# One stage for the projections and the attention of the first block's mixer

## The reference, cut to what matters

```python
def hybrid_mixer(h, w_in, pos_ck, w_ck1, w_ck2, pos_cv, w_cv1, w_cv2, w_out, cos, sin):
    proj = h @ w_in                       # 2840 columns
    q_n, kv_n, gate_n, moba = jnp.split(proj, ...)
    ...
    o_nsa = nsa_mixer(q_n, *kv_n, gate_n, ...)     # 8 heads of 64: compressed, selected, window
    o_moba = moba_mixer(*qkv_m, cos, sin)          # 8 heads of 64
    return jnp.concatenate([o_nsa, o_moba], axis=-1) @ w_out

# nsa_mixer
    kc = gelu((blocks(k_cmp) + pos_ck) @ w_ck1) @ w_ck2    # 15 blocks of 32 tokens, hidden width 256
    vc = gelu((blocks(v_cmp) + pos_cv) @ w_cv1) @ w_cv2
    p_c = masked_softmax(q @ kc.T * scale)
    o = g0 * (p_c @ vc) + g1 * o_slc + g2 * o_win          # both others use rotated q and k
```

## Time and profile before

| | |
|---|---|
| median of 3 runs | 2489.86 us (2486.86 to 2511.51) |
| the profiled execution's own time | 2488.15 us |
| its span, first to last instruction | 2486.4 us |
| PE, PE weight load, DVE, ACT, POOL busy | 2271.5, 2127.8, 1383.4, 980.2, 128.0 us |
| mean granted TensorE clock | 0.943 of full speed |

### The profile page before, as it was taken

How to read it: one execution, slowest core, us unless ns; L and a number is a source line. 1 busy time by engine, 2 the same in 40 slices (tenths; PEclk the granted TensorE clock), 3 DMA queues, 4 the chain that set the end, 5 groups by cost and what they waited for, 6 DMA issues and landing times. The chain is left out here.

```text
span 2486.4 us, 39443 instructions
## 1 busy us (share of the span) xinstructions
PE 2271.5 (91%) x16084; PEld 2127.8 (86%) x16084; DVE 1383.4 (56%) x1944; ACT 980.2 (39%) x1302; POOL 128.0 (5%) x88
## 2 busy tenths in 40 slices
PE   6997999899799899989968989988997989988998
PEld 6997987799799798779958979987997979987997
DVE  5544424654555451455527566557665856656765
ACT  4333324433433241543325433345544542334543
POOL 0001430000000053000000010000000010000000
PEclk9998979999899896999989989998998999998999
DMA  7433410643454351055325322336534322235551
GB/s 265 193 135 129 157 68 1 264 169 134 180 202 169 107 195 68 1 207 196 147 93 187 110 81 86 102 102 251 193 124 154 136 89 75 97 96 195 211 188 57
DMA packets 79565, 349.02 MB, mean 140 GB/s; under 512 B 21185, under 2 KB 30529, under 8 KB 45505
## 3 DMA queue, kind: packets, MB, share of 16 engines
q1 hardware_dynamic: 79424, 347.07, 38.4%
HBM read 345.99 MB, written 1.05 MB: 140 GB/s over the span
## 5 line engine op out<-in xcount | busy, mean ns | idle before, releaser
L88 PE MATMUL bank<-ffn_hT_split,ffn_split_weights 128*128 128x256 f32 x1408 | 402.1, 286 | 11.7 <-DVE ffn_hT_split L174 11.7
L89 PE MATMUL bank<-ffn_hT_split,ffn_split_weights 128*128 128x256 f32 x1408 | 401.7, 285 | 0.0
L90 PE MATMUL bank<-ffn_hT_split,ffn_split_weights 128*128 128x256 f32 x1408 | 401.6, 285 | 0.0
L88 PEld LDWEIGHTS bank<-ffn_hT_split,ffn_split_weights 128*128 128x128 f32 x1408 | 273.6, 194 | 14.2 <-DVE ffn_hT_split L174 12.8
L89 PEld LDWEIGHTS bank<-ffn_hT_split,ffn_split_weights 128*128 128x128 f32 x1408 | 273.6, 194 | 1.4
L90 PEld LDWEIGHTS bank<-ffn_hT_split,ffn_split_weights 128*128 128x128 f32 x1408 | 273.6, 194 | 0.0
L88 PE MATMUL bank<-conv_ffn_hT_split,conv_ffn_split_weights 128*128 128x256 f32 x704 | 201.3, 286 | 5.5 <-DVE conv_ffn_hT_split L174 5.5
L90 PE MATMUL bank<-conv_ffn_hT_split,conv_ffn_split_weights 128*128 128x256 f32 x704 | 200.9, 285 | 0.0
L89 PE MATMUL bank<-conv_ffn_hT_split,conv_ffn_split_weights 128*128 128x256 f32 x704 | 200.9, 285 | 0.0
L339 DVE TENSOR_TENSOR ffn_split_weights<-ffn_arrived_gate_up,ffn_split_weights 128x2048 fp32r<-128x2048 f32 x84 | 188.8, 2288 | 21.3 <-ACT ffn_split_weights L269 21.3
L1288 DVE TENSOR_TENSOR mix_parts<-mix_arrived,mix_parts 128x1024 fp32r<-128x1024 f32 x88 | 107.3, 1224 | 137.6 <-ACT mix_parts L1283 137.4
(11 more groups left out here) (365 smaller groups left out, 5825.8 us busy)
## 6 DMA issues: line engine op xcount, KB each, us to landing
ffn_arrived_gate_up<-in_ffn SPq DMA_DIRECT2D x88, 1024.0 KB, 8.2
ffn_arrived_down<-in_ffn SPq DMA_DIRECT2D x44, 1024.0 KB, 4.9
mix_arrived<-in_mix_w SPq DMA_DIRECT2D x88, 512.0 KB, 3.5
conv_ffn_arrived_gate_up<-in_conv_ffn SPq DMA_DIRECT2D x44, 1024.0 KB, 6.7
rw_project_arrived<-in_w_in SPq DMA_DIRECT2D x34, 1024.0 KB, 5.0
project_arrived<-in_w_in SPq DMA_DIRECT2D x22, 1024.0 KB, 6.9
conv_ffn_arrived_down<-in_conv_ffn SPq DMA_DIRECT2D x22, 1024.0 KB, 4.9
attend_arrived<-in_w_out SPq DMA_DIRECT2D x8, 1024.0 KB, 5.9
```

What stands on the lines that cost most here:

```text
L88: pe.matmul(out, lhs[0], rhs[0], start=start, stop=False)
L89: pe.matmul(out, lhs[0], rhs[1], start=False, stop=False)
L90: return pe.matmul(out, lhs[1], rhs[0], start=False, stop=stop)
```

## The change

`project_phase` and `attend_phase` become one phase, `nsa_phase`, with one set of semaphores, one ring over 16 units (12 of w_in, 4 of w_out), and buffers at fixed places. The barrier between the two is gone.

- The columns to be compressed become jobs 0 to 3, the queries jobs 4 to 7. Only jobs 0 to 11 run ahead of the attention. After each of jobs 8 to 11 stands a quarter of the hidden layers (16 matmuls, two passes each).
- w_cmp1 is loaded behind units 3 and 4, the position table behind unit 1.
- Jobs 12 to 21 are cut into 24 pieces of 12 matmuls, which stand ahead of score(u) in steps 0 to 31, but for every fourth. The compressed part (L994 and its softmax) is spread over steps 1 to 24.
- The units' order is branch by branch, first tile 0 and 1 of branches 1 and 2, then the second mixer's heads of both tiles. The output product is 32 groups of three matmuls: 15 stand in steps 34 to 41 and 44 to 50, 17 behind the loop. o is turned in four parts, three of them in the loop.
- The filler matmuls of `keep_clock` are gone from the mixer.
- The rotation (three operations for each rotated job) is done by VectorE, and the high and low parts of w_out by ScalarE and VectorE; GpSimd keeps a memset.
- All transposes of probabilities go to one bank instead of two, so turn(u) waits for pT_ready >= u, that is for copy_probs(u-1), where it waited for copy_probs(u-2).

```diff
+    jobs = [(j // 2, j % 2 * P, "plain", CMP_T + j) for j in range(4)]
+    jobs += [(2 + j // 2, j % 2 * P, "rotate", Q_T + j) for j in range(4)]
     jobs += [(4, 0, "rotate", KS_T), (4, P, "rotate", KW_T), (5, 0, "tokens", 0), (5, 0, "tokens", 1)]
     jobs += [(6 + j // 2, j % 2 * P, "rotate", MQ_T + j) for j in range(8)]
     jobs += [(10 + half, 0, "values", 1 + half) for half in range(2)]
...
+    def job_of_piece(p):
+
+        return (JOBS_FIRST + p // 2, p % 2 == 1) if p < 16 else (20 + (p - 16) // 4, p % 4 == 3)
...
+    PIECE_AT = {u: p for p, u in enumerate(u for u in range(MOBA) if u % 4 != 3)}
+    ENDS_AT = {u: job_of_piece(p)[0] for u, p in PIECE_AT.items() if job_of_piece(p)[1]}
+    SWAP_AT = {u + 1: job for u, job in ENDS_AT.items() if job < 20}
+    O_TURN = {31: 0, 39: 1, 46: 2}
+    READ_AT = {11: (0, 1), 16: (0, 0), 19: (0, 2), 27: (1, 1), 29: (1, 0), 35: (1, 2)}
+    BRANCH_ORDER = list(READ_AT.values())
+    SUM_AT = {21: 0, 37: 1}
+    OUT_STEPS = {34 + n: (0, n // 2, n % 2) for n in range(8)} | {44 + n: (1, n // 2, n % 2) for n in range(7)}
...
         @block.sync
...
-                if n == 2:
+                if n == 1:
...
-                if n == 7:
+                if n in (3, 4):
+                    sp.dma_start(c.wc1[:, n - 3], w_c1[n - 3].rearrange("(j p) n -> p j n", p=P)).then_inc(s["wc1_loaded"], 16)
+                if n == 4:
...
         @block.scalar
...
+            for i in range(JOBS_FIRST):
+                copy_job(i)
+                high_after(i)
...
+            for u in range(N_ATT + 3):
+                if u in ENDS_AT:
+                    copy_job(ENDS_AT[u])
+                if u < N_ATT:
+                    exponent(u)
+                if 2 <= u < N_ATT + 2:
+                    copy_probs(u - 2)
+                if u in ENDS_AT:
+                    high_after(ENDS_AT[u])
+                if u == 8:
+                    act.wait_ge(s["cmp_shifted"], 1)
+                    act.activation(cp, cs, ACT.Exp).then_inc(s["cmp_exp"], 1)
+                if u - 1 in O_TURN:
+                    o_high(O_TURN[u - 1])
+                if u == 48:
+                    ring.high(act, N_UNITS - 1, width(N_UNITS - 1))
+            o_high(3)
...
         @block.vector
...
+            def rotate(i):
+
+                n, to = rotated_jobs.index(i), jobs[i][3]
+                part = c.cos_part[:, n % 2]
+                dve.wait_ge(s["copied"], i + 1)
+                dve.tensor_tensor(part, c.raw[:, to, :], c.cos, ALU.mult)
+                dve.wait_ge(s["swapped"], n + 1)
+                dve.tensor_tensor(c.rot[:, to, :], swap_bank(n)[:, 0:S], c.sin, ALU.mult).then_inc(s["sin_done"], 1)
+                dve.wait_ge(s["sin_done"], n + 1)
+                dve.tensor_tensor(c.rot[:, to, :], c.rot[:, to, :], part, ALU.add).then_inc(s["rotated"], 1)
...
+            for i in range(JOBS_FIRST):
+                if i - 2 in rotated_jobs:
+                    rotate(i - 2)
+                low_after(i)
+                if i == 4:
+                    key_columns()
+            repeat_hidden()
+
+            for u in range(N_ATT + 3):
+                if u < N_ATT:
+                    mask(u)
+                if u == 2:
+                    copy_kv()
+                if u == 7:
+                    compressed_shift()
+                if u == 9:
+                    compressed_sums()
+                if u == 13:
+                    compressed_copy()
+                if u - 1 in SWAP_AT:
+                    rotate(SWAP_AT[u - 1])
+                if u - 1 in ENDS_AT:
+                    low_after(ENDS_AT[u - 1])
+                if u in READ_AT:
+                    gate_weights(*READ_AT[u])
+                if u - 1 in READ_AT:
+                    read_branch(*READ_AT[u - 1])
+                if u in SUM_AT:
+                    sum_branches(SUM_AT[u])
...
+                if u == 49:
+                    ring.low(dve, N_UNITS - 1, width(N_UNITS - 1))
+            moba(1)
...
         @block.tensor
...
+            for i in range(JOBS_FIRST):
+                begin_job(i)
+                if jobs[i][2] == "tokens":
+                    last = token_job(i, jobs[i][3], range(KT), 0)
+                else:
+                    last = turned_job(i, range(KT))
+                last.then_inc(s["projected"], 1)
+                if i - 1 in rotated_jobs:
+                    swap(i - 1)
+                if i >= 8:
+                    last = hidden_columns((i - 8) // 2, i % 2)
+            last.then_inc(s["hid_ready"], 1)
+
+            def half_job(p):
+                job, whole = job_of_piece(p)
+                if p < 16:
+                    if p % 2 == 0:
+                        begin_job(job)
+                    last = turned_job(job, range(p % 2 * 4, p % 2 * 4 + 4))
+                else:
+                    if p % 4 == 0:
+                        begin_job(job)
+                    t = p % 4 // 2
+                    last = token_job(job, t, range(p % 2 * 4, p % 2 * 4 + 4), t * S)
+                if whole:
+                    last.then_inc(s["projected"], 1)
...
             def turn(u):
...
                 t = units[u][0]
                 pe.wait_ge(s["exp_ready"], u + 1)
-                if u >= 2:
-                    pe.wait_ge(s["pT_ready"], u - 1)
+                if u >= 1:
+                    pe.wait_ge(s["pT_ready"], u)
...
+            for u in range(N_ATT + 3):
+                if u in PIECE_AT:
+                    half_job(PIECE_AT[u])
+                if u in OUT_STEPS:
+                    out_rows(*OUT_STEPS[u])
+                if u < N_ATT:
                     score(u)
-                if 2 <= u < len(units) + 2:
+                if 2 <= u < N_ATT + 2:
                     turn(u - 2)
                 if u >= 3:
-                    if (u - 3) % PER_T == 0:
-                        compressed_sum((u - 3) // PER_T)
                     add(u - 3)
...
+                if u in SWAP_AT:
+                    swap(SWAP_AT[u])
+                if u == 1:
+                    compressed_kv()
+                if 3 <= u <= 6:
+                    compressed_scores((u - 3) // 2, (u - 3) % 2)
+                if u == 11:
+                    compressed_turn()
+                if u == 14:
+                    compressed_sum(0)
+                if u == 24:
+                    compressed_sum(1)
+                if u in O_TURN:
+                    turn_o(O_TURN[u])
+            out_rows(1, 3, 1)
+            for k in (4, 5):
+                for half in range(2):
+                    out_rows(0, k, half)
+            turn_o(3)
+            for k in (6, 7):
+                for half in range(2):
+                    out_rows(0, k, half)
+            for half in range(2):
+                for k in range(4, KT):
+                    out_rows(1, k, half)
```

653 lines of the change are left out of this document (327 added, 326 removed).

## The result

The changed kernel takes **2482.45 us** (median of 16 runs, 2476.03 to 2496.07), the kernel before 2510.95 in the same series; the ratio is 0.9923, 95% interval 0.9897 to 0.995. The prediction said 2415 us, with a range from 2398 to 2440. So the kernel became faster by 0.8%, a quarter of the gain that was expected (3.0%), and the result lies outside the range; a result within 1% had been given a chance of 0.04. (The executions of the kernel before fall into two groups, 2487 to 2493 and 2510 to 2517 us, and one of 2536.30 that the ratio leaves out; the ratio fits the means of the others, 2482.9 to 2502.0, and not the medians, since the middle of before lies in its upper group, while the profiled execution, 2488.15, is of the lower.)

A forecast was written before the change was run, and what follows sets the result against it. TensorE's own order was taken as the bound. A mixer: 230.0 - 43.3 saved + 4 waits + 2 head = 192.7 us; two mixers save 74.6 from 2488.15, giving 2413.6, plus 1.7 for the median: 2415 us, range 2398 to 2440.

The forecast's parts named there:

- the part on waits: Mixed steps: masks waiting behind VectorE's rotations and low parts delay TensorE by 4 us a mixer, bounds 0 and 24.
- Hidden layers: Compression's hidden layers: four quarters between dense jobs run at full clock, 24.85 us become 11.1, saving 13.7 a mixer.
- The 19.14 us between: From hidden layers to first score: gelu, barrier and compressed softmax run beside job pieces; 4 us stay, saving 15.1.
- fillers: Attention units with 128 keys: 24 filler matmuls of 0.37 us go, saving 8.9 us a mixer.
- turning of o: After the attention: 6.26 us become 16 transposes between other work, 2.2 us, saving 4.1 a mixer.
- ramp: Filling and emptying of the attention's pipeline: 3.1 us, half covered, saving 1.5 a mixer.
- The head: Mixer's start: unit 5's load lands at about 251 and position additions hold the first swap; 2 us added, bounds 0 and 9.
- Single bank for turned probabilities: Attention: turn waits for the preceding unit's copy, a loop of 1.42 us a unit against 1.39; cost nothing to speak of.
- the one with the clock falling in the quarters: Hidden-layer quarters: each loses some 2 to 2.5 us to a fallen clock, 10 a mixer, 2435 us; chance 0.10.
- VectorE's order decides: Every low part and rotation on VectorE delays TensorE in full, 20 us more a mixer, 2455 us; chance 0.06.
- The mixed stage loses the clock altogether: Steps 0 to 50: without fillers the clock falls, factor 1.64, +75 us a mixer, 2565 us; chance 0.03.
- What would show it: Signs: mixer 193 us, clock 1.00 from second job, no TensorE gap over a microsecond from job 11 through output product.

The follow-up runs named there:

- the last kernel: The kernel with w_out splits on GpSimd and residual additions at step 42, plus rotations one job earlier and tile 0's branch sum at step 24: 2428.16 us, ratio 0.9716.
- the runs with fillers and with bursts: Changed kernel plus one filler product ahead of each score from step 32: 2474.69 us; changed kernel with its 15 output groups in bursts, mostly of four: 2454.13 us.

## Why the prediction was wrong

The direction was right, the size was not: 2415 against 2482. **The step that failed** is in the part on waits: "I take 4, near the lower end". A wait was entered at its own length, and a mixed stage at full clock; against the rival that it loses the clock stood "units with 256 keys ran without a filler at 1.00 throughout". That row showed a stage that kept its clock as long as nothing stopped it, and nothing did stop it. It could not say what a stop costs, nor that a fallen clock comes back there: without the fillers the same units with 256 keys all ran at 1.2 GHz in one mixer. The waits themselves came to 7.1 us in the first mixer, against the 6 taken (4 in the steps, 2 in the head), so their length was nearly right; the clock behind them, entered at nothing, cost some 23.6 us, added up over the windows above as length times what is missing to 1.00 (two of 1.7, 0.2, 10, 1 and 9).

What each run took away, in us (first, second mixer; from single profiled executions, in which falls that the edit doesn't touch come and go by some 2 us each):

| step | mixer | worth |
|---|---|---|
| changed kernel | 223.7, 222.9 | |
| w_out splits to GpSimd | 212.8, 206.6 | 10.9, 16.3 |
| residual additions at step 42 | 201.8, 203.1 | 11.0, 3.6 |
| rotations first, branch sum at 24 | 196.6, 196.0 | 5.2, 7.1 |
| the prediction's sum | 192.7 | 3.9, 3.3 |
| the same without its 6 us of stalls | 186.7 | 9.9, 9.3 |

The last row is the one to compare the last kernel with, since the stalls are gone from it. So the terms of TensorE's own work were 9 to 10 us a mixer too low, and that the last kernel comes within 4 us of 192.7 is in part luck: stalls that it doesn't have stand for work that was sized too small.

Point by point:

- **Hidden layers**: sized 11.1 us, measured 14.6 (4 x 3.65). The mechanism was right, the clock held in all eight quarters (it fell behind one). The pass was mis-sized: "11 to 12 of them fit into a microsecond" came from the counts of windows of 1 us, and such a count takes in the instructions that reach over the window's edges. Inside a quarter of the changed kernel a window of 1 us counts 11 as well, though 32 passes take 3.65 us, 0.114 each. This is 3.5 us of the 9 to 10 in the last row of the table.
- **The 19.14 us between, fillers, turning of o, ramp** (-29.6 together): right in kind; in sum they left too little time, as the last kernel shows. From the score of step 0 to that of step 32 it takes 79.75 us at full clock, where these terms make 75.7 (24 pieces of 1.42, 8 swaps, 16 units of 0.75 and 16 of 1.39, and 4), and from there to the end 47.2 where the sum has some 43; the excess is spread over the steps.
- **The head**: unit 5 was split from 250.5 on, as forecast (about 251), and ScalarE waited 2.6 us for it. The rotation behind the position additions was seen ("hold the first swap by about 1 us"), at half its size (1.94), and without the 3.5 us at half clock. What held it was the low half of unit 5, not the additions: these were done 1.2 us before that low half began.
- **Single bank for turned probabilities**: nothing to speak of, as predicted; the largest wait of that kind without a hold is 0.36 us. The longer ones also end with a copy (L775), but a second bank would hardly have shortened them: the add(u-3) of the same step needs the same copy.
- **Rivals**: the one with the clock falling in the quarters came true behind one of eight quarters here (some 2 us), and at three of eight in the experiment that had them alone. "VectorE's order decides" named the place and priced it by the delay only. "The mixed stage loses the clock altogether" had nearly the right price (a factor of 1.64; a step of one unit and one group takes 2.84 us at 1.2 GHz in the changed kernel and 1.60 at full clock in the last one, 1.78) and the wrong trigger: it asked whether the mixed work is dense enough on average, and would have been decided where "about half of that stage is at 1.2 GHz"; it was some 44 us of 150. The two are one mechanism, short waits from the one and the loss from the other, and neither alone had it. What the prediction took for agreement, the mean of 0.73 around o, has a wait in front of it too: TensorE waited 1.23 us at 414.54, the clock was at 1.00 until then, and at 0.50 from 415 to 418, when the transposes were nearly done. In the last kernel the transposes of o, and the steps with transposes and no dense piece (32, 33, 42 and 43), ran at 1.00. The Trainium skill, "TensorE: Matmul & The Clock Gate", section "HAM oscillation — how this bites in real kernels", which the prediction weighed for the quarters, bears on this place too: it draws pauses for DMA of some 3 to 5 us between bursts. The pauses here are of 0.8 to 1.9 us, shorter than those, and in the first mixer of the changed kernel the clock fell in or close behind each of the four places that had them.
- **What would show it**: "no gap over a microsecond" and "the clock at 1.00" were the right marks. Both are broken in the changed kernel and both are met in the last one.

**Open**: what decides how long the clock stays down (3, 7, 13, 20 or 48 us behind waits of like length, 87 us behind none), and which waits take it. The one of 0.82 us at step 23 did in both mixers of the changed kernel, and in neither mixer of the runs with fillers and with bursts. One of 1.2 us at the same step did in one mixer and not in the other, in two kernels. One of 1.46 us at step 44 did in one of two, and waits of 1.28, 1.73 and 1.78 us at the first swaps had no fall directly behind them (two of these had one some 8 us later, behind the first quarter). All nineteen waits of 1.94 us or more behind the second job had one.

## What to carry to other kernels

When work is woven together to fill an engine, price each remaining wait of TensorE not at its length but at its length and the half clock behind it, until something dense comes; here 7 us of waits brought 24 us more. A wait of a microsecond doesn't always take the clock, so a single good execution doesn't clear it. Look at the granted clock, not the busy share, which was 100% in the long slow stretches. Then go back along the waits: the cure was to move single operations of the in-order engine by one step (a pair of additions by one step, 11 us), and to keep long ones such as a 2.3 us split off the engine on which the masks wait. Where a filler is removed, ask what it was keeping up.

## What the runs showed of the hardware

- A wait of TensorE of 1.36 us between mixed, narrow steps took the clock to 1.2 GHz, in both mixers; one of 0.30 us at the same place did not, in both. In between it isn't the length alone: of six waits of 0.82 us at one step two did, of four of 1.2 us two did, and of three of 1.73 to 1.94 us at the swaps one did directly.
- At 1.2 GHz, matmuls without a gap did not bring it back for 20 and 48 us when the dense groups came one a step (with four groups, 12 matmuls of 128x512, in a row and the same work around them, the stretches at 1.2 GHz were 7 us or less). Units with 256 keys and nothing dense between them stayed at 1.2 GHz to their end in one mixer, and at 2.4 GHz in the kernel before.
- Thirty-two passes of 30 columns between dense jobs were followed by, or ran into, 3 to 7 us at 1.2 GHz in four of sixteen cases, without a wait before.
- An addition of 512 columns with both operands in SBUF took 4.88 us on VectorE in place of 0.69 while GpSimd subtracted 2048 columns (4.83 us).
- One matmul of 128x128 against the identity in each unit of 1.12 us held the clock of before in both mixers (in the kernel with the quarters alone it was lost in such units once, for some 7 us); without it the same units ran at 1.2 GHz for 45 us, with TensorE busy throughout.
